# Two layers of a transformer-like model on one core: gates and output product of the second layer as split products, weight high parts on GpSimd, small results in PSUM

## What is computed

```python
h = _rmsnorm(x, norm_g[1])                     # the rows called x1 in the kernel
qc, kv..., gates, zc, qd, kd, vd, zd = _split(h @ o_w_in, ODD_SIZES)
...
y_c = _nsa_attention(qc, ...)                  # units "c" (three branches: compressed, selected, window)
y_d = _banded_attention(qd, kd, vd, ..., sink) # units "d" (window of 128, with sinks)
y = concat(y_c * silu(zc), y_d * silu(zd))
x = x + y @ w_out[1]                           # wo1_0 to wo1_3 in the kernel
```

## Time and profile before

| | |
|---|---|
| median of 3 runs | 909.24 us (907.1 to 910.63) |
| the profiled execution | 910.96 us, its span 909.2 us, mean PE clock 0.994 |
| PE busy | 882.9 us (97%), 6792 matmuls |
| DVE / ACT / POOL busy | 428.8 / 446.7 / 609.0 us |
| DMA | 177.61 MB, mean 195 GB/s |

### The profile page before, as it was taken

How to read it: one execution, slowest core, us unless ns; L and a number is a source line. 1 busy time by engine, 2 the same in 40 slices (tenths; PEclk the granted TensorE clock), 3 DMA queues, 4 the chain that set the end, 5 groups by cost and what they waited for, 6 DMA issues and landing times.

```text
span 909.2 us, 16515 instructions
## 1 busy us (share of the span) xinstructions
PE 882.9 (97%) x6792; PEld 826.0 (91%) x6792; DVE 428.8 (47%) x952; ACT 446.7 (49%) x665; POOL 609.0 (67%) x485
## 2 busy tenths in 40 slices
PE   6999999899999999999999999999999999999997
PEld 5898889897777999888988799999999999999996
DVE  3998665743875466882445232331124562211001
ACT  3434667344555453354444547586334775533330
POOL 0766468740000669989777777768889999997880
PEclk9999999999999999999999999999999999999999
DMA  9844577783210279597666444444536655545421
GB/s 347 344 146 158 214 243 266 252 307 131 100 48 1 93 275 391 219 376 261 226 213 232 149 176 145 154 167 156 216 139 232 231 185 187 185 141 186 185 94 47
DMA packets 27907, 177.61 MB, mean 195 GB/s; under 512 B 3080, under 2 KB 5780, under 8 KB 7480
## 3 DMA queue, kind: packets, MB, share of 16 engines
q1 hardware_dynamic: 26248, 174.35, 53.1%
q10 hardware_dynamic: 1584, 2.20, 0.7%
HBM read 174.95 MB, written 3.43 MB: 196 GB/s over the span
## 4 chain that ended last, share of the span: by engine, by line
PE 90%; DVE 4%; ACT 2%; issue 1%; DMA 1%; POOL 1%; ACTq 0%; DVEq 0%; SPq 0%
PE proj L742 18%; PE proj L744 18%; PE proj L745 18%; PE proj L717 5%; PE proj L822 3%; PE proj L819 3%; PE proj L821 3%; PE proj L1016 3%; PE proj L778 2%; PE mixed L968 1%; PE proj L1089 1%; PE transposed L937 1%; PE scores L923 1%; PE mixed L951 1%; PE sums L876 1%
## 5 line engine op out<-in xcount | busy, mean ns | idle before, releaser
L656 POOL TENSOR_TENSOR w_lo<-raw,w_hi 128x512 fp32r<-128x512 f32 x328 | 418.9, 1313 | 208.2 <-ACT w_hi L1374 208.1
L744 PE MATMUL proj<-parts,w_lo 128*128 128x256 f32 x952 | 266.4, 280 | 0.6 <-POOL w_lo L656 0.6
L742 PE MATMUL proj<-parts,w_hi 128*128 128x256 f32 x904 | 257.3, 285 | 0.5 <-POOL w_lo L656 0.3
L745 PE MATMUL proj<-parts,w_hi 128*128 128x256 f32 x904 | 252.6, 279 | 0.0
L1374 ACT ACTIVATE w_hi<-raw 128x2048 fp32r<-128x2048 f32 x82 | 156.8, 1914 | 112.4 <-DMA raw<-in_weights 61.0
L744 PEld LDWEIGHTS proj<-parts,w_lo 128*128 128x128 f32 x952 | 179.1, 188 | 1.7 <-POOL w_lo L656 0.8
L742 PEld LDWEIGHTS proj<-parts,w_hi 128*128 128x128 f32 x904 | 169.9, 188 | 2.8 <-issue 2.1
L745 PEld LDWEIGHTS proj<-parts,w_hi 128*128 128x128 f32 x904 | 170.4, 188 | 0.0
L656 POOL TENSOR_TENSOR w_lo<-arena,w_hi 128x512 fp32r<-128x512 f32 (+2 forms) x44 | 56.2, 1317 | 56.5 <-ACT w_hi L1374 56.5
L742 PE MATMUL proj<-hid_hi,w_hi 128*128 128x256 f32 x160 | 45.3, 283 | 0.0
L819 PE MATMUL proj<-w_hi,parts 128*128 128x512 f32 x112 | 45.0, 402 | 0.0
(11 more groups left out here) (402 smaller groups left out, 2111.7 us busy)
## 6 DMA issues: line engine op xcount, KB each, us to landing
raw<-in_weights SPq DMA_DIRECT2D x105, 1024.0 KB, 5.0
arena<-in_weights SPq DMA_DIRECT2D x32, 1024.0 KB, 7.2
wide<-in_weights SPq DMA_DIRECT2D x9, 1024.0 KB, 7.0
probT<-in_weights SPq DMA_DIRECT2D x8, 1024.0 KB, 5.6
dil_lines<-dil_line SPq DMA_DIRECT2D x1, 2304.0 KB, 12.9
prob<-in_weights SPq DMA_DIRECT2D x2, 1024.0 KB, 4.9
dil_bias<-dil_lines SPq DMA_DIRECT2D x1, 1536.0 KB, 9.4
xT<-in_x SPq DMA_DIRECT2D x2, 512.0 KB, 5.8
```

Source lines behind the costliest of these rows:

```text
L656: nc.gpsimd.tensor_tensor(lo_slots[RAW_AT[n]][:, at], raw_slots[RAW_AT[n]][:, at], hi_slots[HI_AT[m]][:, at].bitcast(F32), ALU.subtract).t ...
L742: nc.tensor.matmul(dst, whi, h, start=first, stop=False)
L744: nc.tensor.matmul(dst, wlo, h, start=False, stop=False)
L745: last = nc.tensor.matmul(dst, whi, lo[:, k, :], start=False, stop=stop)
```

## The change

1. zc0, zc1 join the split units in the usual way (high parts on ACT). zd0, zd1 and wo1_0 to wo1_3 ("PLACED") are split too, but their high parts are made by POOL, four copies of a quarter each, before POOL makes their low parts. ACT's `passing` skips them.
2. The gated results of the second layer, four pieces of 512 columns, are split: high parts by ACT (pieces 0 and 1 in units 12 and 13, 2 and 3 after the attention), low parts of 0 and 1 by POOL ahead of wo1_3, of 2 and 3 by DVE. wo1_0 and wo1_1 become one `two_units` product: piece 0 in unit 13, piece 1 in unit 14, 2 and 3 after the attention.
3. In PSUM instead of SBUF: the softmax factor and the negated maximum of units c and d (bank `st`), the first layer's gated results (`y_bank`), the layer norm's mean and factor, and the normed rows x1 (`h_bank`, two pieces in each of four banks).
4. Slots and order of loads: wo1_0, ak2_0 use a fifth high slot (`w_hi_b`, over `dil_bias`); ak2_0, ak2_1 and rq0 are loaded in their natural order, behind wo1_3.

In the diff `high` is a function of POOL's program, `H:` a branch of PE's, `gathered_high` is ACT's and `low(k)` DVE's.

```diff
+PLACED = ("zd0", "zd1", *(f"wo1_{i}" for i in range(4)))
-    "zd1.1.1", "", "H:wo1_0 E:zd1", "H:wo1_1", "")]
+    "zd0.1", "zd1.0 E:zd0", "", "zd1.1.0", "zd1.1.1", "L:y0", "H:0 E:zd1 L:y1", "H:1", "")]
-SPLIT_SOON = [..., "qd0", "qd1", "kd"]
+SPLIT_SOON = [..., "qd0", "qd1", "kd", "zc0", "zc1", *PLACED]
-    return EARLY if n >= WEIGHT_AT["wo1_0"] else [*range(NRAW), *EARLY]
+    return [*range(NRAW), *EARLY]
+SHARED_HI = SPLIT[SPLIT_AT["wo1_0"]:SPLIT_AT["ak2_1"] + 1]
-for _us, _before in ((BEFORE_NORM["x2"], "wo1_2"), (("rq0",), "wo1_3"), ...
+for _us, _before in (...
+        def y_bank(c):
+            return (st, pt, sc[0], sc[1])[c]
+        def h_bank(k):
+            return (sc[0], sc[1], pt, po)[k % 4][:, S * (k // 4):S * (k // 4) + S]
...
+            def high(u):
+                pool.wait_ge(proj_ready, GROUP_AT["zc0"] + 1 if u == SHARED_HI[0] else LAST_READ[SPLIT[HI_BEFORE[m]]] + 1)
+                pool.wait_ge(raw_in[RAW_AT[n]], raw_target(n))
+                for at in quarters(u):
+                    nc.gpsimd.tensor_copy(hi_slots[HI_AT[m]][:, at], raw_slots[RAW_AT[n]][:, at]).then_inc(sem("hi_pool"), 1)
...
+                if u == "wo1_3":
+                    for n in range(2):
+                        pool.wait_ge(y_hi, 4 + n + 1)
+                        nc.gpsimd.tensor_tensor(fl(parts[:, 1, 2 * n:2 * n + 2]), fl(yT1[:, 2 * n:2 * n + 2]), ..., ALU.subtract) \
+                            .then_inc(sem("y_low_pool"), 1)
+                if u in PLACED:
+                    high(u)
                 low(u)
...
                 elif name[:2] == "H:":
-                    output_half(name[2:], 0, yT1, y_of)
+                    n = int(name[2:])
+                    state["pair"] = two_units(("wo1_0", "wo1_1"), gathered(n, n + 1), state["pair"] if n else None, done=False)
+            def gathered(lo, hi):
+                return [((2 * n, 2 * n + 1), every, lambda k, n=n: pe.wait_ge(*((sem("y_low_pool"), n + 1) if n < 2 else (y_ready, n + 3)))) for n in range(lo, hi)]
...
-                    output_half(f"wo1_{i}", 1, yT1, y_of)
-                else:
-                    plain(f"wo1_{i}", yT1)
+                    two_units(("wo1_0", "wo1_1"), gathered(2, 4), state["pair"])
+                elif i > 1:
+                    project(f"wo1_{i}")
...
+            def gathered_high(n):
+                operand_high([(hi_of(n), two(yT1, n), [(proj_ready, GROUP_AT["zd1"] + 1), (po_free, STEPS_TO["b"] + 2 * n + 2)])])
...
                 def low(k):
-                    dve.wait_ge(h_hi, KD * (n - 1) + k + 1)
+                    dve.wait_ge(h_hi, KD * (n - 1) + k + 1 + 4 * (n == 1 and k < 4))
...
+                    if n == 1 and k >= 4:
+                        dve.wait_ge(h_hi, k - 3)
...
-                own.did(V.tensor_reduce(s[:, 0:4], e[:, :, 0:n], AX.X, ALU.max, negate=True))
+                top = st[:, S + 12 + 4 * (u % 3):S + 12 + 4 * (u % 3) + 4]
+                own.did(V.tensor_reduce(top, e[:, :, 0:n], AX.X, ALU.max, negate=True))
...
-                own.did(V.tensor_tensor(cut(s[:, 4:8], 2), cut(s[:, 0:4], 2), down, ALU.min))
+                own.did(V.tensor_tensor(cut(top, 2), cut(top, 2), down, ALU.min))
                 own.settle()
+                own.did(V.tensor_copy(s[:, 4:8], top))
...
+                factor = s[:, 8:8 + m] if part in "ab" else st[:, S + 4 * (u % 3):S + 4 * (u % 3) + 4]
-                own.did(V.reciprocal(s[:, 8:8 + m], s[:, 8:8 + m]))
+                own.did(V.reciprocal(factor, s[:, 8:8 + m]))
...
-                V.tensor_tensor(e[:, :, 0:n], e[:, :, 0:n], s[:, 8:12].unsqueeze(2).broadcast_to([P, 4, n]), ALU.mult) \
+                V.tensor_tensor(e[:, :, 0:n], e[:, :, 0:n], factor.unsqueeze(2).broadcast_to([P, 4, n]), ALU.mult) \
...
-            narrow_attention(PART["c"] + PART["d"], FILL_CD, 1)
+            narrow_attention(PART["c"] + PART["d"], FILL_CD, 1, lambda: parts_low(yT1, [2]))
+            parts_low(yT1, [3])
```

More of the change, by code:

```diff
@@ L63 @@
 FILL_CD = [x.split() for x in (
-    "N:kd E:zc0", "zc1.0 E:kd", "zc1.1", "E:zc1", "modA zd0.0.0", "zd0.0.1 E:modA", "", "zd0.1", "zd1.0 E:zd0", "", "zd1.1.0",
-    "zd1.1.1", "", "H:wo1_0 E:zd1", "H:wo1_1", "")]
+    "N:kd E:zc0", "zc1.0 E:kd", "zc1.1", "E:zc1", "modA zd0.0.0", "zd0.0.1 E:modA", "",
+    "zd0.1", "zd1.0 E:zd0", "", "zd1.1.0", "zd1.1.1", "L:y0", "H:0 E:zd1 L:y1", "H:1", "")]
+PLACED = ("zd0", "zd1", *(f"wo1_{i}" for i in range(4)))
 HEAD_B, HEAD_CD = ["bv1", "sp_bk1", "zb0"], ["vc2", "zc0", "sp_kd"]
@@ L156, in last_in @@
     return [g for g in BANKED[:FILL_AT[group]] if BANK_OF[g] == b][-1]
-SPLIT_SOON = ["bq1", "bk0", "bk1", "bv0", "bv1", "zb0", "zb1", "za0", "za1"] + [f"wo0_{i}" for i in range(4)] + ["kcvc", "kskw", "vsvw", "qc0", "qc1", "vdgt", "qd0", "qd1", "kd"]
+SPLIT_SOON = ["bq1", "bk0", "bk1", "bv0", "bv1", "zb0", "zb1", "za0", "za1"] + [f"wo0_{i}" for i in range(4)] + ["kcvc", "kskw", "vsvw", "qc0", "qc1", "vdgt", "qd0", "qd1", "kd", "zc0", "zc1", *PLACED]
 SPLIT = [u for u in WEIGHTS if u in SPLIT_SOON or WEIGHT_AT[u] >= WEIGHT_AT["ak2_0"] and u[:2] != "ad"]
@@ L207 @@
 LOADS = [u for u in WEIGHTS if u not in ADA_FIRST + ADA_VECTOR + ADA_LATE]
-for _us, _before in ((BEFORE_NORM["x2"], "wo1_2"), (("rq0",), "wo1_3"), *(((u,), before) for u, before in zip(ADA_FIRST, FIRST_BEFORE)), *(((u,), before) for u, before in zip(ADA_LATE, LATE_BEFORE)),
+for _us, _before in (*(((u,), before) for u, before in zip(ADA_FIRST, FIRST_BEFORE)), *(((u,), before) for u, before in zip(ADA_LATE, LATE_BEFORE)),
                      *(((u,), before) for u, before in zip(ADA_VECTOR, ("rk0", "rk1", "rk2", "rk3", "rv0a", "rv2a", "rv2b", "rv3a")))):
@@ L1356, in _, with passing @@
             state = dict(hi=0)
-            def passing(name, most=len(SPLIT)):
-                while state["hi"] < min(len(SPLIT), most):
+            def passing(name):
+                while state["hi"] < len(SPLIT):
                     m = state["hi"]
@@ L1474, in between @@
                         fl((yT0 if name[1] == "b" else yT1)[:, (0 if name[1] == "c" else 4) + 2 * i:][:, 0:2])
-                    nc.scalar.activation(dst, ready(name)[:], ACT.Tanh, scale=0.5).then_inc(sem("z_tanh"), 1)
+                    nc.scalar.activation(dst, ready(name, name not in PLACED)[:], ACT.Tanh, scale=0.5).then_inc(sem("z_tanh"), 1)
+                elif name[:3] == "L:y":
+                    gathered_high(int(name[3:]))
                 elif name == "L:centre":
@@ L1672, in _ @@
             narrow_attention(PART["c"] + PART["d"], FILL_CD)
+            for n in (2, 3):
+                gathered_high(n)
             table(ACT.Sqrt)
@@ L1984, in between @@
                     dve.wait_ge(sem("ln_sqrt"), 1)
-                    own.did(V.reciprocal(rstd[:, 0:S], rstd[:, 0:S]))
+                    own.did(V.reciprocal(st[:, 0:S], rstd[:, 0:S]))
                     own.settle()
-                    V.tensor_tensor(y_a, y_a, every(rstd[:, 0:S]), ALU.mult).then_inc(sem("ln_scaled"), 1)
+                    V.tensor_tensor(y_a, y_a, every(st[:, 0:S]), ALU.mult).then_inc(sem("ln_scaled"), 1)
                 elif name[:2] == "rg":
@@ L2124, in _, with convolved_low @@
             score_max(PART["b"][1])
+            def convolved_low(pieces):
+                operand_low([(two(parts[:, 1], c), y_bank(c)[:], two(parts[:, 0], c)) for c in pieces])
             def conv_end():
-                parts_low(yT0, Y_ORDER[:1])
+                convolved_low(Y_ORDER[:1])
                 for c in range(2):
-                    y = wide[:, 1024 + 512 * c:1536 + 512 * c]
+                    y = y_bank(c)[:]
                     dve.wait_ge(sem("ln_silu"), 2 * c + 2)
```

72 lines of the change are left out of this document (42 added, 30 removed).

## The result

The changed kernel takes 913.47 us (median of 13 runs, 910.91 to 916.57); the kernel before, run beside it, 909.67 us (13 runs, 906.94 to 913.1). The ratio is 1.0038, 95% interval 1.0021 to 1.0056: slightly slower, within the 0.5% that was called no change. Forecast were 902.5 us and a range up to 908. The profiled execution of the changed kernel took 911.31 us (span 909.5), that of before 910.96 (span 909.2).

The account below looks back on a forecast made before the run. PE, busy 97% of the span, was taken as the bound, DVE as the attention's second. Gains of 4.1 + 1.9 + 0.35 + 0.3 = 6.65 us, say 6.7, off the 909.24 us median gave 902.5 us; range 899 to 908.

Parts of the forecast that it names:

- part C: Second layer's attention: of 6.6 us leaving PE, 0.3 us come through; ends 2.1 gained and 1.1 lost.
- The first rival: Attention: DVE-POOL meetings cost 2.6 us more, another low-clock stretch 1.7; 906.8 us, no tellable change; 17%.
- the estimate of 0.65 us: DVE against POOL: an operation arriving at random waits half a POOL instruction, making part C 0.15 us worse.
- Part D: Output product behind the attention: 144 split matmuls take 16.8 us instead of 20.92, gaining 4.1 us.
- Part B: Normed rows x1: low parts finish 2.3 us sooner, PE's waits nearly go; 1.9 us gained, ends 1.0 and 2.1.
- Part A: First layer's gated results: the last two low parts get faster; 0.35 us gained, ends 0 and 0.5.
- the third rival: More comes through: no meeting costs anything (1.8 us), no low-clock stretch at 274 us (1.7 us); 899.0 us; 8%.
- the low-clock stretch at 274 us: Attention: a stretch of low PE clock, priced at 1.7 us, that the third rival has not coming.
- the walk: Part C's step-by-step offsets along the attention against the old times: 0.3 us gained, 2.1 with no meeting.
- POOL keeps up: Attention: POOL's added low parts and copies, at 0.8 us a copy, finish before PE wants them; cost nothing.
- POOL is late: Attention: with copies at 2.6 us, PE stands at H:0, 16 us are lost, 918.5 us; 6%.
- Behind 326 us: Long stretch to 860 us: PE hardly waits, so what is saved ahead of it should arrive at the end.

Follow-up runs that it names:

- e6: e5 with the second layer's normed rows x1 put back in SBUF: 904.59 us, 0.9946 of the kernel before.
- e5: e1 with the gain also going through PSUM and the last part's sum written to the factor's place in PSUM: 901.61 us, 0.9914 of the kernel before.
- e1: The changed kernel with the attention's maximum with 1e-30 written to PSUM instead of back into SBUF: 908.02 us, 0.9988 of the kernel before.
- e10: e9 with each added instruction on 128x256 elements instead of 128x4, and the one ahead of the first normalisation left out: 907.63 us, 0.9978.
- e4: The changed kernel with POOL waiting once, ahead of zd1's third low part, until DVE has made the third unit's probabilities: 907.97 us, 0.9987.
- e3: The changed kernel with POOL waiting once, ahead of wo1_0's high parts, until DVE has made the third unit's probabilities: 908.1 us, 0.9989.
- e8: The changed kernel with POOL waiting once, ahead of zd1's high parts, until DVE has made the second unit's probabilities: 910.71 us, 1.0005.
- e9: The changed kernel with added 128x4 TENSOR_TENSORs in SBUF, at about 216.8 us and in eight normalisations: 913.23 us, 1.0075 of the kernel before.

## Why the prediction was wrong

**The step that failed** stands in part C: "L1903 and L1968, which read only `stat` or `mod`. I take 0.6 us for each, ends 0 and 1.1". That both would meet POOL was right. The upper end was the wait for one instruction of POOL, taken from rows in which DVE meets POOL again and again. L1903 came after 17 gapless instructions of POOL and took 10.85 us, 9.6 us above that end. The first rival ("meetings and a further low-clock stretch") had the right resource and the low clock, but with the price of one instruction: 2.6 us.

The trace of the kernel before already had such a wait, far from the attention. DVE in order of time:

```profile
672.15 4.02 DVE L2369 TENSOR_TENSOR arena<-arena 128x512 f32<-128x512 f32 x1
```

L2369 has both inputs and its output in SBUF, as L2289 of the earlier trace rows, and takes 0.71 us at its shortest. Here it comes at the 14th instruction of a run of POOL's without a gap, from 655.58 to 675.62 us, and ends 0.55 us behind that run. One of its four executions takes 3.95 to 4.39 us in each of the sixteen traces. The prediction took its upper end from L2289, which always follows another meeting.

The Trainium skill ("SBUF — State Buffer", section "Who interferes with whom") says that whoever starts first holds the shared ports for its whole instruction and the other blocks. For one meeting the traces agree (0.35 to 1.25 us for 128x4 elements, ending with POOL's instruction). It doesn't say who is next when POOL's own next instruction is there too; the estimate of 0.65 us took for granted that it was DVE, and the runs show up to 16 instructions of POOL ahead of it. It also says that a two-input instruction with one operand in PSUM, and the reduction, don't contend: here L1927, a reduction of 128x1024 wholly in SBUF, takes 1.22 us beside POOL.

**Part D** was right in kind, 4.1 us predicted, 3.7 measured (25.3 to 21.6 us), PE busy throughout.

**Part B** was undersized: 1.9 us, ends 1.0 and 2.1. The first sums stand at 165.86 instead of 168.80 us in the chain, 2.9 us earlier, 0.56 of it from part A, which leaves 2.4. The waits of 2.1 us went as predicted (the low parts take 0.42 us each, the wait for them is gone). Undone in e6 it costs 3.0 us, but with a low clock behind the waits that the profiled execution of the kernel before, with the same waits, doesn't have:

```profile
160.00:200.00 40.00, 37.64 (x358) 34.95 (x356) 27.30 (x59) 16.41 (x23) 25.80 (x22) 1.00 0.78 271
```

So the waits alone are the term, and the clock comes on top in some executions only.

**Part A**: 0.35 predicted; DVE's first result of the residual stands at 133.72 us instead of 134.28, 0.56 us.

**Part C** without the stalls is e5: the attention takes 77.8 instead of 81.0 us, 3.2 us gained. The prediction had 2.1 "with no meeting at all" and, in the third rival, 1.7 more if the low-clock stretch at 274 us doesn't come. It does come in e5: its 40 mixes take 4.07 us, as before. What is gone is another one, at the start of the attention, where before 16 records of zc took 4.94 us against 3.46 at full clock. PE of before and of e5, in order of time:

```profile
213.91 4.94 PE L1016 MATMUL proj<-dil_bias,raw 128*128 128x256 f32 x16
```

```profile
267.50 4.07 PE L999 MATMUL mixed<-probT,arena 128*64 128x128 f32 x40
```

Those 1.5 us are not shown to come from the change: e1, whose program is the same as e5's up to there, has the low clock at 211 to 214 us. Without them 1.7 us of the 3.2 are left, against 2.1 in the walk. That the third rival's 3.5 us on top of 6.65, 10.1 in all, is also what e5 shows in its span (909.2 to 899.1) is therefore partly luck; by the medians e5 gains 8.1 us. The walk along the stretch is borne out to some tenths of a us in its total, all but the meetings; its single steps weren't tested.

**POOL keeps up**: right. Its copy takes 0.61 us with a pitch of 0.56 (2.29 us for four), where 0.8 was taken:

```profile
L669 POOL CAST w_hi<-raw x12: 606/614/619, 215.1 to 290.2; 128x512 fp32r<-128x512 f32 x12
```

y's low parts follow at 283 and 287 us, the last placed unit is made by 296. The Trainium skill's one-input rule ("GPSIMD Engine Reference", "Engine selection"), an estimate of 0.5 us, was the nearer one. PE never waits for POOL in the attention. The rival "POOL is late" fell; what came true is its mirror image, DVE late because POOL isn't.

**Behind 326 us** nothing was lost, as predicted: 528.66 us of PE's work from 330 to 860.

## What to carry to other kernels

When work moves to an engine that shares ports with another, list every instruction of the other that is left with all operands in SBUF, the 128x4 ones too, and ask how long the first engine will by then have run without a gap: a wait may last as long as the run does. Moving one of them only hands the wait to the next, as e1 showed; a cheap way round is PSUM, as the output of an instruction with one input or as one input of an instruction with two; for the maximum and the gain here that was worth 1.3% against the changed kernel. PSUM as output alone doesn't help an instruction with two inputs in SBUF (L1948). A pause in the run must come within few instructions of each meeting.

## What the runs showed of the hardware

- DVE's TENSOR_SCALAR (4 elements and more), SCALAR_TENSOR_TENSOR and TENSOR_TENSOR with all operands in SBUF wait for POOL; a TENSOR_TENSOR with both inputs in SBUF waits with PSUM as output too (0.51 and 0.61 instead of 0.16 us in e5). TENSOR_SCALAR to PSUM, two-input instructions with one input in PSUM, RECIPROCAL, the reduction, and TENSOR_SCALAR with one element took their usual 0.15 to 1.22 us beside it.
- At the 4th to 10th instruction of a gapless run of POOL such an instruction got the next turn (the 10th in e10, without an earlier meeting). At the 11th and later, without an earlier meeting, it never did in nine cases in the attention (3.15 to 15.07 us; where e4's first came at the 18th, it took 1.27 us, until POOL was made to pause), nor did L2369 of before at the 13th or 14th, with 128x512 elements, in any of the sixteen traces. Whether the number of instructions counts or the time is open: the 10th came 8.8 us behind the start of the run, the 11th 9.7 us.
- DVE gets in when POOL pauses (0.77 us in e3, 0.84 in e4). Behind a pause of 1.75 us (e8), and behind meetings in which DVE itself works for 0.4 us (e10), a later one got the next turn again; behind meetings of 0.15 us (e9) it didn't, nor at the 11th and 14th instruction behind the pauses of 0.84 and 0.77 us. That fits a lead of POOL's which grows over a run and is used up when it is held back, and e10 was forecast by it. The lead itself no trace shows; nor was the shortest pause that is enough tried, nor why the limit lies between 10 and 11.
